# Moving the transposed activations within SBUF: four buffers at 96, 32, 160 and 224 bytes past a multiple of 256

## The reference

```
# first block
h = rms_norm(x, pre_mix_norm);  proj = h @ w_in            # 2048 x 5656
mix = concat(diff_attention(...), nsa_attention(...))      # 256 x 2048
x = x + rms_norm(mix @ w_out, post_mix_norm)
h = rms_norm(x, pre_ffn_norm)
u = causal_dwconv(h @ w_up, conv_w, conv_b)                # w_up 2048 x 11264
x = x + rms_norm((gelu(gate) * up) @ w_down, post_ffn_norm)
# second block
proj = rmsnorm(x, mix_pre_gain) @ w_in_2                   # 2048 x 5376
x = x + rmsnorm(concat(window_attention, hgrn2) @ w_out_2, mix_post_gain)
u = relu(rmsnorm(x, mlp_pre_gain) @ w_up_2)                # 2048 x 8192
x = x + rmsnorm((u * u) @ w_down_2, mlp_post_gain)
```

## Time and profile before

| | |
|---|---|
| median of three runs | 2247.35 us |
| the profiled execution | 2246.66 us |
| its span, first to last instruction | 2244.8 us |
| TensorE busy | 2219.1 us, 99% of the span |
| VectorE, ScalarE busy | 63%, 50% |
| granted TensorE clock over the span | 0.999 |
| HBM read | 414.85 MB, 186 GB/s |

### The profile page before, as it was taken

One profiled execution on the slowest core, in us unless ns is written; L12 is line 12 of the kernel. 1 busy time (PEld: TensorE's weight loads), 2 busy tenths in 40 slices (PEclk: granted clock), 3 DMA queues, 4 the chain that ended last, 5 costly groups with the idle time before them and its releaser, 6 DMA issues.

```text
span 2244.8 us, 34148 instructions
## 1 busy us (share of the span) xinstructions
PE 2219.1 (99%) x12721; PEld 1889.8 (84%) x12721; DVE 1415.7 (63%) x1826; ACT 1118.4 (50%) x1566; POOL 65.6 (3%) x95
## 2 busy tenths in 40 slices
PE   8999999999999999999999999999999999999998
PEld 6888888888888888888888888888888888888887
DVE  5567685677776447777575786657666444666545
ACT  5455464555555445555454654545444444444443
POOL 4100000000000000000000000000000000000000
PEclk9999999999999999999999999999999999999999
DMA  9954455566565666666657555566666666666663
GB/s 280 318 179 138 133 163 183 155 196 199 176 205 189 196 190 187 185 195 196 208 149 203 145 160 159 177 193 167 198 189 188 196 193 191 189 191 190 212 192 112
DMA packets 321663, 418.84 MB, mean 187 GB/s; under 512 B 13566, under 2 KB 233048, under 8 KB 320788
## 3 DMA queue, kind: packets, MB, share of 16 engines
q1 hardware_dynamic: 316548, 398.81, 58.5%
q0 software_dynamic: 4720, 16.49, 2.6%
q10 hardware_dynamic: 288, 2.10, 0.2%
HBM read 414.85 MB, written 2.49 MB: 186 GB/s over the span
## 4 chain that ended last, share of the span: by engine, by line
PE 95%; DVE 2%; DMA 1%; ACT 1%; issue 1%; POOL 0%; POOLq 0%; DVEq 0%; ACTq 0%
PE PS L2012 25%; PE PS L2016 13%; PE PS L1899 10%; PE PS L1901 10%; PE PS L1900 10%; PE PS L2084 5%; PE PS L2355 3%; PE PS L2087 2%; PE PS L2100 2%; PE PS L2102 2%; PE PS L2101 2%; PE PS L2358 2%; PE PS L2368 1%; PE PS L2370 1%; PE PS L2369 1%
## 5 line engine op out<-in xcount | busy, mean ns | idle before, releaser
L2012 PE MATMUL PS<-actT,whi 128*128 128x512 f32 x2432 | 759.0, 393 | 0.0
L2016 PEld LDWEIGHTS PS<-actT,wlo 128*128 128x128 f32 x2432 | 457.2, 188 | 103.6
L1214 DVE TENSOR_TENSOR wlo<-stage,whi 128x1024 fp32r<-128x1024 f32 x296 | 360.2, 1223 | 219.6 <-ACT whi L780 219.3
L1186 DVE TENSOR_TENSOR wlo<-stage,whi 128x1024 fp32r<-128x1024 f32 x245 | 298.9, 1225 | 302.2 <-ACT whi L722 302.2
L2016 PE MATMUL PS<-actT,wlo 128*128 128x256 f32 x2432 | 479.5, 279 | 0.0
L780 ACT ACTIVATE whi<-stage 128x1024 fp32r<-128x1024 f32 x296 | 311.6, 1058 | 307.3 <-PE PS L2016 294.0
L722 ACT ACTIVATE whi<-stage 128x1024 fp32r<-128x1024 f32 x245 | 258.7, 1060 | 345.6 <-PE PS L1901 322.1
L2012 PEld LDWEIGHTS PS<-actT,whi 128*128 128x128 f32 x2432 | 366.2, 188 | 0.7 <-issue 0.4
L1900 PE MATMUL PS<-wlo,gT 128*128 128x512 f32 x864 | 336.1, 389 | 0.0
L1901 PE MATMUL PS<-whi,gT 128*128 128x512 f32 x864 | 336.1, 389 | 0.0
L1899 PE MATMUL PS<-whi,gT 128*128 128x512 f32 x864 | 336.1, 389 | 0.0
(11 more groups left out here) (334 smaller groups left out, 2478.1 us busy)
## 6 DMA issues: line engine op xcount, KB each, us to landing
stage<-in_w_up SPq DMA_DIRECT2D x304, 512.0 KB, 4.1
stage<-in_w_down SPq DMA_DIRECT2D x216, 512.0 KB, 4.2
stage<-in_w_in SPq DMA_DIRECT2D x160, 512.0 KB, 3.8
stage<-in_w_out SPq DMA_DIRECT2D x64, 512.0 KB, 4.3
stage<-in_w_in SPq DMA_DIRECT2D x16, 256.0 KB, 2.9
DQK<-in_cmp_k_w POOLq DMA_DIRECT2D x8, 512.0 KB, 7.2
DQK<-in_cmp_v_w POOLq DMA_DIRECT2D x8, 512.0 KB, 6.3
stage<-in_w_in SPq DMA_DIRECT2D x8, 280.0 KB, 8.3
```

Of the source, the lines that this page charges most:

```text
L1186: nc.vector.tensor_tensor(wlo[:, s % SPLITS, 0:wd], stage[:, s % STAGES, 0:wd], whi[:, s % SPLITS, 0:wd].bitcast(F32), ALU.subtract).then_ ...
L1214: nc.vector.tensor_tensor(wlo[:, j % SPLITS, :], stage[:, j, :], whi[:, j % SPLITS, :].bitcast(F32), ALU.subtract).then_inc(ev("lo_done"), 1)
L2012: nc.tensor.matmul(o, whi[:, j % SPLITS, at], actT[:, k, :], start=k == 0, stop=False)
L2016: last = nc.tensor.matmul(o[:, S:2 * S], wlo[:, j % SPLITS, at], actT[:, k, 0:S], start=False, stop=k == KC - 1)
```

## The change

`actT` is gone. Each phase has a buffer of its own, and all four lie over each other in one region, each behind a filler of another size. With the small tensors allocated first and `vc4`, `ones`, `gates` moved into `mixer1`, the region begins at 64 modulo 256 (byte 110912), so the buffers start, modulo 256, at:

| phase | filler | buffer | start mod 256 |
|---|---|---|---|
| 1, `in1` and `out1` | 32 | `act1` | 96 |
| 2, `up1` | 224 | `actu1` | 32 |
| 3, `in2` and `out2` | 96 | `act2` | 160 |
| 4, `up2` | 160 | `actu2` | 224 |

What is allocated behind them on the mixers' stacks moves with them: `DQK` and all others of phase 1 from 0 (some from 192) to 32 bytes more, `win` and all others of phase 3 to 160. `yacc`, `gT1`, `gT2` and `pre` stay where they were, by a filler `act_place`. No instruction, semaphore or wait is added or removed, and none changes its order or its shape.

```diff
-        vc4 = sb("vc4", [P, NKV, P])
-        ones = sb("ones", [P, P])
-        gates = sb("gates", [P, TT, GATES])
-        actT = sb("actT", [P, KC, 2 * S], F32R)
...
         mixer1 = ExitStack()
+        sb("behind1", [P, 32 // 4], F32, mixer1)
+        act1 = sb("act1", [P, KC, 2 * S], F32R, mixer1)
+        vc4 = sb("vc4", [P, NKV, P], F32, mixer1)
+        ones = sb("ones", [P, P], F32, mixer1)
+        gates = sb("gates", [P, TT, GATES], F32, mixer1)
...
         mixer2 = ExitStack()
+        sb("behind2", [P, 96 // 4], F32, mixer2)
+        act2 = sb("act2", [P, KC, 2 * S], F32R, mixer2)
...
+        up1 = ExitStack()
+        sb("behind_up1", [P, 224 // 4], F32, up1)
+        actu1 = sb("actu1", [P, KC, 2 * S], F32R, up1)
+        up1.close()
+        up2 = ExitStack()
+        sb("behind_up2", [P, 160 // 4], F32, up2)
+        actu2 = sb("actu2", [P, KC, 2 * S], F32R, up2)
+        up2.close()
+        acts = {"n1": act1, "mix1": act1, "n2": actu1, "n3": act2, "mix2": act2, "n4": actu2}
         ffn = ExitStack()
+        sb("act_place", [P, KC * 2 * S + 1728 // 4], F32R, ffn)
...
-                                nc.tensor.matmul(o, whi[:, j % SPLITS, at], actT[:, k, :], start=k == 0, stop=False)
+                                nc.tensor.matmul(o, whi[:, j % SPLITS, at], (actu1 if name.startswith("up1") else actu2)[:, k, :], start=k == 0, stop=False)
...
-            held_tiles("out1", actT, REGION1_TILES - 8)
+            held_tiles("out1", act1, REGION1_TILES - 8)
```

More of the change, by code:

```diff
@@ L768, in split_turned @@
                     act.wait_ge(ev("turned_" + turn), c // 2 + 1)
-                    nc.scalar.activation(actT[:, c, 0:S], PS[:, banks[c // 2], (c % 2) * S:(c % 2 + 1) * S], ACT.Copy,
+                    nc.scalar.activation(acts[turn][:, c, 0:S], PS[:, banks[c // 2], (c % 2) * S:(c % 2 + 1) * S], ACT.Copy,
                                          scale=gain_of(turn, c)).then_inc(ev("acthi_" + turn), 1)
@@ L946, in branch_high @@
                     act.wait_ge(ev("branch_sum"), h + 1)
-                    nc.scalar.activation(actT[:, h, 0:S], branch_out[:, h, :], ACT.Copy).then_inc(ev("acthi_mix1"), 1)
+                    nc.scalar.activation(act1[:, h, 0:S], branch_out[:, h, :], ACT.Copy).then_inc(ev("acthi_mix1"), 1)
             def diff_high(p):
@@ L953, in diff_high @@
                 for c in (2 * p, 2 * p + 1):
-                    nc.scalar.activation(actT[:, HN + c, 0:S], PS[:, DIFF_BANK[p], c % 2 * S:(c % 2 + 1) * S], ACT.Copy,
+                    nc.scalar.activation(act1[:, HN + c, 0:S], PS[:, DIFF_BANK[p], c % 2 * S:(c % 2 + 1) * S], ACT.Copy,
                                          scale=gain_of("mix1", c)).then_inc(ev("acthi_mix1"), 1)
@@ L1310, in split_turned @@
                     dve.wait_ge(ev("acthi_" + turn), c // 2 * 2 + 2)
-                    nc.vector.scalar_tensor_tensor(actT[:, c, S:2 * S], PS[:, banks[c // 2], (c % 2) * S:(c % 2 + 1) * S],
-                                                   gain_of(turn, c), actT[:, c, 0:S].bitcast(F32),
+                    nc.vector.scalar_tensor_tensor(acts[turn][:, c, S:2 * S], PS[:, banks[c // 2], (c % 2) * S:(c % 2 + 1) * S],
+                                                   gain_of(turn, c), acts[turn][:, c, 0:S].bitcast(F32),
                                                    ALU.mult, ALU.subtract).then_inc(ev("actlo_" + turn), 1)
@@ L1539, in diff_low @@
                 for c in (2 * p, 2 * p + 1):
-                    nc.vector.scalar_tensor_tensor(actT[:, HN + c, S:2 * S], PS[:, DIFF_BANK[p], c % 2 * S:(c % 2 + 1) * S],
-                                                   gain_of("mix1", c), actT[:, HN + c, 0:S].bitcast(F32),
+                    nc.vector.scalar_tensor_tensor(act1[:, HN + c, S:2 * S], PS[:, DIFF_BANK[p], c % 2 * S:(c % 2 + 1) * S],
+                                                   gain_of("mix1", c), act1[:, HN + c, 0:S].bitcast(F32),
                                                    ALU.mult, ALU.subtract).then_inc(ev("actlo_mix1"), 1)
@@ L1601, in branch_low @@
                 for h in (2 * i, 2 * i + 1):
-                    nc.vector.tensor_tensor(actT[:, h, S:2 * S], branch_out[:, h, :], actT[:, h, 0:S].bitcast(F32), ALU.subtract)\
+                    nc.vector.tensor_tensor(act1[:, h, S:2 * S], branch_out[:, h, :], act1[:, h, 0:S].bitcast(F32), ALU.subtract)\
                         .then_inc(ev("actlo_mix1"), 1)
@@ L2015, in one @@
                                 at = slice(c * FW + f * P, c * FW + (f + 1) * P)
-                                last = nc.tensor.matmul(o[:, S:2 * S], wlo[:, j % SPLITS, at], actT[:, k, 0:S],
+                                last = nc.tensor.matmul(o[:, S:2 * S], wlo[:, j % SPLITS, at], (actu1 if name.startswith("up1") else actu2)[:, k, 0:S],
                                                         start=False, stop=k == KC - 1)
@@ L2083, in in1_tile @@
                             o, at = PS[:, bank + f, :], slice(c * FW + f * P, c * FW + (f + 1) * P)
-                            nc.tensor.matmul(o, whi[:, s, at], actT[:, at_k, :], start=at_k == 0, stop=False)
+                            nc.tensor.matmul(o, whi[:, s, at], act1[:, at_k, :], start=at_k == 0, stop=False)
                         for f in range(2):
                             o, at = PS[:, bank + f, :], slice(c * FW + f * P, c * FW + (f + 1) * P)
-                            last = nc.tensor.matmul(o[:, S:2 * S], wlo[:, s, at], actT[:, at_k, 0:S], start=False, stop=at_k == KC - 1)
+                            last = nc.tensor.matmul(o[:, S:2 * S], wlo[:, s, at], act1[:, at_k, 0:S], start=False, stop=at_k == KC - 1)
                 else:
@@ L2098, in tok_tile @@
                         o = PS[:, bank + t, 0:wd]
-                        ah, al = actT[:, at_k, t * P:(t + 1) * P], actT[:, at_k, S + t * P:S + (t + 1) * P]
+                        ah, al = act1[:, at_k, t * P:(t + 1) * P], act1[:, at_k, S + t * P:S + (t + 1) * P]
                         nc.tensor.matmul(o, ah, h, start=at_k == 0, stop=False)
@@ L2354, in in2_tile @@
                             o, at = PS[:, banks[f], :], slice(c * FW + f * P, c * FW + (f + 1) * P)
-                            nc.tensor.matmul(o, whi[:, s, at], actT[:, at_k, :], start=at_k == 0, stop=False)
+                            nc.tensor.matmul(o, whi[:, s, at], act2[:, at_k, :], start=at_k == 0, stop=False)
                         for f in range(2):
                             o, at = PS[:, banks[f], :], slice(c * FW + f * P, c * FW + (f + 1) * P)
-                            last = nc.tensor.matmul(o[:, S:2 * S], wlo[:, s, at], actT[:, at_k, 0:S], start=False, stop=at_k == KC - 1)
+                            last = nc.tensor.matmul(o[:, S:2 * S], wlo[:, s, at], act2[:, at_k, 0:S], start=False, stop=at_k == KC - 1)
                 else:
@@ L2366, in in2_tile @@
                             o = PS[:, banks[t], 0:wd]
-                            ah, al = actT[:, at_k, t * P:(t + 1) * P], actT[:, at_k, S + t * P:S + (t + 1) * P]
+                            ah, al = act2[:, at_k, t * P:(t + 1) * P], act2[:, at_k, S + t * P:S + (t + 1) * P]
                             nc.tensor.matmul(o, ah, h, start=at_k == 0, stop=False)
@@ L2522, in last_turned @@
                         turn_mix2(p)
-            tok("out2", actT, turned="mix2", between=last_turned)
+            tok("out2", act2, turned="mix2", between=last_turned)
             passage("out2", "n4")
```

## The result

The changed kernel takes 2262.79 us (median of three, 2261.24 to 2263.43) against 2247.35 before: ratio 1.0066, 95% interval 1.0053 to 1.008. It is slower by 15.4 us; the forecast was 7.4 us faster, and the time lies just above the range. The profiled execution has a span of 2261.6 us, 16.8 more than before's.

A forecast was written before the change was run, and what follows sets the result against it. The prediction took TensorE's number of matmuls times their pace as the bound. Its six terms for sets and triples summed to -7.4 us, from the median 2247.35 to 2240 us, with a range of 2226 to 2262.

The forecast's parts named there:

- the narrow triples: The 96 triples of 256 or 280 columns: either way by at most 1 us, taken as 0.
- the interpolation: Losses per 1536 columns at D 32, 96, 160, 224 read between four traced points on a 256-byte circle: 3.5, 10, 15, 6 ns.
- `up1`, D = 32: 704 sets (four feat matmuls, 1536 columns each) in `up1`, D 192 to 32: loss 12.5 to 3.5 ns, -6.3 us.
- `up2`, D = 224: 512 four-matmul feat sets in `up2`, D 192 to 224: loss falls from 12.5 to 6 ns, -3.3 us.
- `in1` set, D = 96: 256 four-matmul feat sets in `in1`, D 192 to 96: loss falls from 12.5 to 10 ns, -0.6 us.
- `in2` set, D = 160: 192 four-matmul feat sets in `in2`, D 192 to 160: loss rises from 12.5 to 15 ns, +0.5 us.
- phase 1 triple, D = 160: 192 full-width tok triples with stationary activations in `in1` and `out1`, D 64 to 160: loss 7 to 15 ns, +1.5 us.
- phase 3 triple, D = 96: 256 full-width tok triples with stationary activations in `in2` and `out2`, D 64 to 96: loss 7 to 10 ns, +0.8 us.
- the 280-column block: Only traced odd multiple of 32, D = 160: second half of a tile 0.78 us for six matmuls, first half 0.76.
- The odd start as a price of its own: Rival, chance 0.31: each of 6656 feat matmuls pays 2.5 ns, 16.6 us in all; 2254.3 us, or 2264.
- Placement isn't the cause: Rival, chance 0.17: the losses hang on load order or something else, and the time stays at 2247.4 us.
- the conflict vanishes at odd distances: Rival, chance 0.12: in all phases 1664 sets gain 12.5 ns and 448 triples 7 ns, 23.9 us; 2223.5 us.

The follow-up runs named there:

- The sweep: A kernel without the computation, running only TensorE's sets and triples at all 64 pairs of operand starts: 680 to 703 ns a triple, 690 to 707 a set.
- the exchanged places: The changed kernel with the activations starting at 160, 224, 96, 32 in place of 96, 32, 160, 224 in the four phases: 2263.0 us.

## Why the prediction was wrong

**What held.** TensorE's pace bounds the kernel, and what a set gains or loses arrives in the time one to one, in both directions. The pace depends on D, the distance modulo 256 (to a few ns); the counts of sets and triples were right; the guess that the two 512-column matmuls of a set last 388 and 398 ns is what the trace before shows; the narrow triples moved by 0.5 us, within the 1 us allowed; the down stages stayed at 389 ns; the mixers' other tensors cost nothing that can be seen.

**The step that failed** is the interpolation: "I interpolate round the circle of 256 bytes". It took four points, two of sets and two of triples, as points of one smooth curve. The sweep shows two curves, and neither is smooth: neighbours 32 bytes apart differ by up to 19 ns (a triple at 0 and 32), and sets and triples at one distance differ by up to 16.5 (at 0). The zero of the curve, 680 at D = 0, was a triple's; a set costs 697 there, so the fall toward it that gave `up1` and `up2` their gain didn't exist.

| term | predicted loss, ns | measured, ns | predicted, us | measured, us |
|---|---|---|---|---|
| `up1`, D = 32 | 3.5 | 13.4 | -6.3 | +0.1 |
| `up2`, D = 224 | 6 | 22.7 | -3.3 | +4.8 |
| `in1` set, D = 96 | 10 | 25.4 | -0.6 | +2.9 |
| `in2` set, D = 160 | 15 | 23.4 | +0.5 | +1.7 |
| phase 1 triple, D = 160 | 15 | 22.6 | +1.5 | +3.0 |
| phase 3 triple, D = 96 | 10 | 20.1 | +0.8 | +3.4 |

At D = 160 there was a row, and the forecast averaged it away: the 280-column block gave a loss of 17 to 25 ns, the forecast took 15, and a triple lost 22.6.

The range didn't follow from its own bounds either. With the 30 ns a set that the text gives as the upper bound, 1664 sets lose 17.5 ns more than the 12.5 of before, some 29 us, and the time would be 2276; the range stopped at 2262, below even the 2264 of its own rival. The largest loss measured for a set in the kernel was 25.4.

The prediction had the warning in hand: the 256-column block ran in two rhythms at one address, and the text said that the map isn't smooth. It should have cost the forecast its narrow terms. What could be read without a curve was that the three even distances lose between 0 and 12.5 ns, and that the only odd one lay 10 to 18 ns above its neighbour; that row was right.

**The rivals.** The odd start as a price of its own came nearest in time (2254 to 2264) and is refuted as a mechanism: at distance 0 two odd starts cost 681 or 697 ns like two even ones. It hit because all four new distances are odd, and odd distances are slow for both kinds, but for sets at 32. "Placement isn't the cause" is refuted by the exchanged places. That the conflict vanishes at odd distances is refuted too; all gains are at even ones.

The Trainium skill's rule that TensorE's two read ports are independent and wait for no one ("SBUF — State Buffer", "Who interferes with whom") doesn't describe these float32r streams: with nothing else running, a triple takes 680 or 703 ns by the two starts alone. The measurement decides.

The Trainium skill's cachelines of 16 bytes (the same page, "Specifications (TRN2)") agree with one part of the sweep only. Activations 16 bytes on, weights at 0, take 696.6 ns a set, as at 0, but 8 bytes on they take 706.6 and 4 bytes on 716.6. Elsewhere 16 bytes more do cost, though the start is still a multiple of 16: 703.4 at 80 against 690.0 at 64, and 700.1 at 48 against 693.4 at 32.

**What stays open** is the mechanism. That the two reads hinder each other is inferred from the dependence on the difference of their starts. Not known is why the set's fast and slow matmuls share a line at equal starts, why 320 columns are free of it and 448 are slow at equal starts, why one distance can settle at two paces, why fewer stationary columns don't help. No run here settles it, and a rule for another pattern can't be derived from these.

## What to carry to other kernels

Where TensorE is busy without a gap, group its matmuls by form and operands and compare the distances between their starts: if one instruction has two paces in two places, the placement in memory is a suspect that costs nothing to change. Don't interpolate over addresses: measure each place, with the kernel's own sequence of matmuls, in a small kernel that runs TensorE alone; the map made in that way forecast a gain of 5.3 us where 5.4 were measured, with misses of 1 to 2 us in two stages. Measure it at the kernel's own width too, since the best distance at 512 columns is among the worst at 448. And don't judge by a group's mean over stages, which here stayed at 393 ns while one stage lost 9 ns a set and the other none.

## What the runs showed of the hardware

- A float32r matmul's pace depends on the starts of its two operands by their difference modulo 256 bytes: 680 to 703 ns for a triple, 690 to 707 for a set of the same 1536 columns, with all other engines idle. The width counts too: at 320 columns there is no difference, and at 448 equal starts are slow.
- Most steady sums lie near steps of 3.3 ns above 680, which is 8 cycles at 2.4 GHz: 680, 687, 690, 693, 697, 700, 703, 707, 713.
- Even the best is above the columns alone: 226.6 ns for 512 columns at granted clock 1.00 (2.4 GHz), which is 544 cycles. At 320, 384 and 448 columns the best (146.6, 173.3 and 199.8 ns) is also some 32 cycles above the columns; at 256 it is 16 (113.4 ns).
